# Two chained transformer blocks on one core: order of ScalarE's and VectorE's work in the second block's mixer

## What is computed

```python
h = _rmsnorm(x, norm_mix_g)
c_q, c_kv, k_r, x_m, z, i_pre, f_pre = _split_in(h @ w_in)
q  = (_rmsnorm(c_q, q_norm_g) @ w_uq)            # 8 heads, 64 + 32 rotated
kv = (_rmsnorm(c_kv, kv_norm_g) @ w_ukv)
attn_out = _mla_attention(q_nope, q_rope, k_nope, k_rope, v)
xc = silu(_causal_conv(x_m, conv_w, conv_b))
hm = _mlstm_chunkwise(xc @ w_mq, xc @ w_mk, x_m @ w_mv, ig, fg)   # 4 heads of 128
hm = (hm - mu) * rsqrt(var + EPS) * mh_norm_g
ml_out = (hm + ml_skip * xc) * silu(z)
x = x + concatenate([attn_out, ml_out]) @ w_o
x = x + _hier_moe(_rmsnorm(x, norm_ffn_g), ...)   # 32 experts, top 2
```

## Time and profile before

| | us |
|---|---|
| median of 3 runs | 1010.97 (1010.72 to 1012.38) |
| the profiled execution, own time | 1011.97 |
| its span, first to last instruction | 1010.4 |
| PE busy | 955.8 (95%) |
| DVE busy | 635.3 (63%) |
| ACT busy | 534.4 (53%) |
| mean granted PE clock | 0.991 |

### The profile page before, as it was taken

One profiled execution on the slowest core, in us unless ns is written; L12 is line 12 of the kernel. 1 busy time (PEld: TensorE's weight loads), 2 busy tenths in 40 slices (PEclk: granted clock), 3 DMA queues, 4 the chain that ended last, 5 costly groups with the idle time before them and its releaser, 6 DMA issues.

```text
span 1010.4 us, 14997 instructions
## 1 busy us (share of the span) xinstructions
PE 955.8 (95%) x5635; PEld 733.8 (73%) x5635; DVE 635.3 (63%) x1392; ACT 534.4 (53%) x973; POOL 84.1 (8%) x97
## 2 busy tenths in 40 slices
PE   6999899999999999999999999999899999987796
PEld 5777588888888877688888888867676665443355
DVE  4679768999945566768999945667876221110046
ACT  5757667676634565767666644765742211100054
POOL 0100001122100302001122101010000000000000
PEclk9999999999999999999999999999899999999998
DMA  8934246655565544246655664414577999999971
GB/s 272 384 131 126 91 125 200 202 177 180 200 204 173 203 146 146 84 138 197 204 171 188 199 184 142 149 48 167 209 305 306 396 419 420 421 420 421 421 280 44
DMA packets 99359, 224.58 MB, mean 222 GB/s; under 512 B 9535, under 2 KB 64210, under 8 KB 86994
## 3 DMA queue, kind: packets, MB, share of 16 engines
q1 hardware_dynamic: 99122, 223.04, 61.8%
q10 hardware_dynamic: 160, 0.53, 0.2%
HBM read 222.50 MB, written 1.05 MB: 221 GB/s over the span
## 4 chain that ended last, share of the span: by engine, by line
PE 76%; DMA 10%; DVE 8%; ACT 3%; SPq 2%; issue 1%; DVEq 0%; ACTq 0%
PE ps L559 72%; DMA ringx<-in_w_up_e_dram 6%; PE ps L563 3%; DMA ring<-in_w_up_e_dram 3%; DVE wl L1991 2%; DVE smb L2005 1%; DMA ring<-in_w_uv_dram 1%; SPq L2993 1%; SPq L2996 1%; DMA ring<-in_w_in_even_dram 1%; ACT L1443 1%; ACT wh L1446 0%; DVE pb L1996 0%; ACT hh L1443 0%; DVE x L1991 0%
## 5 line engine op out<-in xcount | busy, mean ns | idle before, releaser
L1991 DVE TENSOR_TENSOR wl<-ring,wh 128x1024 fp32r<-128x1024 f32 (+3 forms) x212 | 268.8, 1270 | 106.6 <-ACT wh L1446 105.3
L1446 ACT ACTIVATE wh<-ring 128x1024 fp32r<-128x1024 f32 (+3 forms) x212 | 222.2, 1051 | 105.6 <-PE ps L559 101.3
L559 PE MATMUL ps<-hx,wh 128*128 128x512 f32 (+1 forms) x720 | 245.0, 387 | 0.1
L559 PE MATMUL ps<-hx,wl 128*128 128x256 f32 x704 | 196.6, 280 | 0.0
L559 PEld LDWEIGHTS ps<-hx,wh 128*128 128x128 f32 x720 | 133.7, 187 | 28.8 <-issue 0.6
L559 PEld LDWEIGHTS ps<-hx,wl 128*128 128x128 f32 x704 | 133.1, 189 | 0.0
L559 PE MATMUL ps<-ring,xg 128*32 128x256 f32 (+1 forms) x592 | 79.4, 388 | 7.2 <-DMA ring<-in_w_gate_e_dram 4.2
L2938 POOL TENSOR_TENSOR fs<-fs,rt 128x256 f32<-128x256 f32 x44 | 52.4, 1213 | 357.1 <-ACT fs L1443 357.1
L559 PE MATMUL ps<-wh,hh 128*128 128x512 f32 (+3 forms) x192 | 79.7, 415 | 2.2 <-DVE wl L1991 2.1
L559 PE MATMUL ps<-wl,hh 128*128 128x512 f32 (+3 forms) x192 | 75.1, 391 | 0.0
L559 PE MATMUL ps<-wh,hl 128*128 128x512 f32 (+3 forms) x192 | 73.0, 388 | 0.0
(11 more groups left out here) (317 smaller groups left out, 1674.8 us busy)
## 6 DMA issues: line engine op xcount, KB each, us to landing
ring<-in_w_up_dram SPq DMA_DIRECT2D x88, 512.0 KB, 4.8
ring<-in_w_down_dram SPq DMA_DIRECT2D x22, 1024.0 KB, 5.0
ring<-in_w_up_e_dram SPq DMA_DIRECT2D x19, 1024.0 KB, 18.1
ring<-in_w_gate_e_dram SPq DMA_DIRECT2D x18, 1024.0 KB, 13.7
ring<-in_w_down_e_dram SPq DMA_DIRECT2D x15, 1024.0 KB, 26.0
ringx<-in_w_down_e_dram SPq DMA_DIRECT2D x14, 1024.0 KB, 21.0
ring<-in_w_in_odd_dram SPq DMA_DIRECT2D x12, 1024.0 KB, 5.2
ringx<-in_w_gate_e_dram SPq DMA_DIRECT2D x12, 1024.0 KB, 15.7
```

The lines of the kernel that those rows point to most:

```text
L559: return e.matmul(o, l, r, start=start, stop=stop)
L1446: return e.activation(o, i, ACT.Copy)
L1991: return e.tensor_tensor(o, a, b, op)
```

## The change

Four places of the mixer get another order; no instruction is added or taken away, and PE's own list stays as it is.

1. DVE: the split of X1 (`split_lo(c_in2[0] + 6)`) moves behind the first step of `side2`, the latent norm.
2. ACT: `swish(0)` moves behind the read-outs of `q2T`.
3. DVE, loop: the split of Z2 moves from step 0 to step 2. At step 11 the read-out of the mLSTM bank moves ahead of the split of O1. At step 13 `mix_lo` of the second latent output moves ahead of step 3 of the mLSTM norm.
4. ACT, loop: the silu of z moves from step 12 to step 11, the split of O2 from step 11 to 12 and that of O3 from step 13 to 14, `mix_hi` of the second latent output from behind the loop to step 13 ahead of the norm's root, and the scaling of the convolution by the skip gain from step 11 to 13 behind the root.

```diff
-            swish(0)
             for i in (1, 3):
                 evac(flat(qT3[0:96, 2 * i:2 * i + 2, :]), "q2T", i, rows=96)
+            swish(0)
...
                     copy(mix[:, 1, 512:1024], b[:, :]).then_inc(of(drained, "ml", 1), 1)
+                    for m in range(4):
+                        emptied(q, "z", m)
+                    act(szT[:, :, :], szT[:, :, :], ACT.Silu).then_inc(s_sz, 1)
+                if i == 12:
+                    next(outp)
+                if i == 13:
+                    warm()
+                    mix_hi("mla", 1, mla_hi[:, 1, :])
+                    q.wait_ge(s_var, RV["mln"])
+                    act(st[:, 16:24], st[:, 8:16], ACT.Sqrt).then_inc(s_std, 1)
                     q.wait_ge(s_xc, 2)
                     for h in range(4):
                         act(xcT[:, h, :], xcT[:, h, :], ACT.Copy, scale=gain("sk2", h))
-                if i == 12:
-                    for m in range(4):
-                        emptied(q, "z", m)
-                    act(szT[:, :, :], szT[:, :, :], ACT.Silu).then_inc(s_sz, 1)
-                    warm()
-                if i == 13:
-                    q.wait_ge(s_var, RV["mln"])
-                    act(st[:, 16:24], st[:, 8:16], ACT.Sqrt).then_inc(s_std, 1)
-                if i in out_at[2]:
-                    next(outp)
...
-            mix_hi("mla", 1, mla_hi[:, 1, :])
+                if i in (13, 14):
+                    next(outp)
+            next(outp)
...
             tok_evac("pj", pj[:, 0, :], "nm2", 424)
-            split_lo(c_in2[0] + 6, wh, wl)
...
             next(side)
+            split_lo(c_in2[0] + 6, wh, wl)
...
+                if i == 11:
+                    next(hms)
+                if i == 2:
+                    next(proj)
+                    next(proj)
                 if i and i - 1 in z_steps and i != 10:
                     next(proj)
                 if i == 11:
+                    next(proj)
+                if i == 12:
                     next(hms)
-                    next(proj)
-                if i in (12, 13):
+                if i == 13:
+                    mix_lo("mla", 1, mla_hi[:, 1, :], mla_lo[:, 1, :], 10)
                     next(hms)
-                if i == 14:
-                    mix_lo("mla", 1, mla_hi[:, 1, :], mla_lo[:, 1, :], 10)
                 if i == 0:
-                    next(proj)
-                    next(proj)
                     gate_rows(0)
```

## The result

| | before | after |
|---|---|---|
| median of 5 runs, us | 1011.13 (1010.72 to 1012.38) | 1015.82 (1012.52 to 1016.82) |
| ratio, 95% interval | | 1.0043 [1.0032, 1.0053] |
| the profiled execution, own time and span | 1011.97, 1010.4 | 1012.52, 1010.9 |

What follows compares the result with a forecast made beforehand. PE holds 76% of the chain of waits; from 766 us DMA is full. From 1011.97, 3.4 + 1.8 - 1.65 - 1.5 = plus 2.05 gave 1014.0; half of 1.00 off made 1013.5, range 1010.6 to 1016.4.

Steps and rivals of the forecast that it cites:

- X1, plus 3.4: At X1 behind the latent norm: PE waits 4.2 us for the later split, reaching the latents' transposes 3.4 us later.
- The rival in which PE finds X1 ready: At X1: the moved split isn't waited for, so the kernel gets faster, 1007.6 us; chance 0.03.
- The clock behind it, plus 1.8 between 0 and 3.05: Behind PE's wait at X1: the clock falls to half and costs 1.8 us, bounds 0 and 3.05.
- The rival in which the clock holds: At X1: no clock drop follows the wait, so the 1.8 us goes, 1011.7 us; chance 0.18.
- The swish, nothing: Silu behind the read-outs of q's transposes: no effect, as the silus run under PE's z product.
- Z2, minus 1.65: First loop steps: without DVE's 7.06 us stand, PE's second mLSTM score comes sooner, gaining 1.65 us, between 1.2 and 1.9.
- The half-limit: At the second mLSTM score: the moved Z2 split ends near 684.0, so the next maxima start about 0.25 us late.
- The loop's end, minus 1.5: Last value product to O4: PE's 2.89 us wait and its clock drop go, but the norm limits the gain to 1.5.
- The rival of a second drop: Ahead of O3 and O4: new waits of 1.3 and 1.9 us, clock drop adding 1.76 to 3.05, about 1015.9; chance 0.14.
- Paid in full: Loop's end: all 5.9 us kept instead of 1.5, DVE's O4 split near 721, 1009.1 or 1007.3 us; chance 0.08.
- The table loads: ACT's two switches: 1.28 us per load counted; the skill page's drains, 2.8 us more and near 1016, left out.
- One for one to the end: From 766 us the DMA engines are full, so every microsecond at PE's last mixer product reaches the end.

Runs made afterwards that it cites:

- only_x1_busy: Kernel before with only the split of X1 moved behind the latent norm, plus 32 extra products on PE ahead of X1; 1013.46 us, ratio 1.0030.
- only_x1: Kernel before with only the split of X1 moved behind the latent norm; 1017.26 us, ratio 1.0064.
- after_again: The whole change, unaltered, measured once more against the kernel before; 1014.20 us, ratio 1.0039.
- only_z2: Kernel before with only the split of Z2 moved from step 0 to step 2 of the loop; 1007.26 us, ratio 0.9972.
- only_swish: Kernel before with only `swish(0)` moved behind the read-outs of `q2T`; 1011.50 us, ratio 0.9998.
- only_end: Kernel before with only the reordering at the loop's end, on ACT and DVE; 1011.60 us, ratio 1.0008.
- undo_x1: The change with the split of X1 put back ahead of the latent norm, the other three edits kept; 1009.35 us, ratio 0.9985.
- after_busy: The whole change plus 32 extra products on PE ahead of X1; 1012.69 us, ratio 1.0013.
- only_end_keep: Kernel before with only the loop's end reordered, plus three more wide products on PE ahead of the router's; 1013.93 us, ratio 1.0031.

## Why the prediction was right, step by step

The forecast was slower, 1013.5 in a range of 1010.6 to 1016.4. The medians 1015.82 and 1014.20 lie in the range, 2.3 and 0.7 above the forecast. The direction is earned: X1 alone makes the kernel slower, and putting X1 back makes the change faster than before. That the sum comes so close is in part luck. By the medians of the kernels with one edit, X1 costs 6.44 (5.2 forecast with its clock), Z2 gains 3.56 (1.65), the loop's end costs 0.64 where it was to gain 1.5, the swish costs 0.54 (0); the last two are no change by their intervals. Two terms are off by about 2 us in opposite directions. The step that failed is the loop's end.

- *X1, plus 3.4*: right. only_x1_busy, with the clock kept up, has 3.36. The wait was 4.06 (4.2 forecast). The rival in which PE finds X1 ready falls.
- *The clock behind it, plus 1.8 between 0 and 3.05*: right in kind and near in size. It cost 2.33 in the first profile and in only_x1, and 4.86 - 3.36 = 1.5 in after_again, where the stretch was shorter. The rival in which the clock holds falls for these three executions. One reading behind this term was wrong: the trace of before does have a wait longer than 4.2 us before the experts, PE's first one, 6.26 us for a load at the start of the program. The products of 128x484 behind it take about 0.60 us each until 15 us and 0.38 from there on. The trace's record of the clock begins only at 15.15 us, so that wait could give the term no bound.
- *The swish, nothing*: right.
- *Z2, minus 1.65*: right. The first profile has 4.31 - 5.99 = -1.68 from z's first product, and only_z2 -1.74. The half-limit I worked out is there too: the second score at 688.33, the next maxima just behind the moved split.
- *The loop's end, minus 1.5*: the mechanism was wrong. The size was right up to 745 us, by luck (-1.62 in the first profile, -1.57 in after_again, from 712), and so was the order of the steps: against the shift of 3.84 that the stage started with, DVE took O4's split at 725.09 (725.08 before). ACT's four durations, added from 719.9, make 725.4 and not the 725.1 of the prediction; they overlap a little, and ACT was done at 728.89 - 3.84 = 725.05. But I put the gain down to the order, which brings 0.1 us. only_swish shows nearly all of the 1.6 without the new order, as the price of the drop at 719. And in only_end, undo_x1, after_busy and after_again the clock falls again at 745 to 752 and takes 1.7 back.
- *The rival of a second drop* was right about the new waits (1.3 and 1.9 us forecast, 1.05 and 1.61 measured), about the price (1.76 at its lower end, 1.7 measured) and the sequel, wrong in part about the place: behind O4's wait in undo_x1 alone, and in four kernels of the new order at the router, where PE waits just 0.4 us. I gave it 0.14, which was too little. With it and the measured clock, 3.36 + 2.33 - 1.68 - 1.6 + 1.7 = 4.1, against 4.7 and 3.4 measured.
- *Paid in full*: falls. It asked for DVE's O4 split near 721 us, and that split did not move.
- *The table loads*: the Trainium skill (ScalarE: Activation LUTs, section What ACT_TABLE_LOAD costs) adds a drain of about 1.38 us to a switch. The trace does not agree: after the loads at 715.52 and 719.59 the next instruction starts 1.29 and 1.30 us later, the load's own 1.28, and the copies ahead of the loads end at 715.50 and 719.58: no drain shows. That 1014 to 1016 came out is no evidence for it.
- *One for one to the end*: not borne out in single executions. From 766 to 990 us the shift changes by -1.4 us in the first profile, +0.4 in after_again and -2.6 in undo_x1, though the transfers fill that stretch. About 1.55 of it is the wait of 2.89 for one expert load that the profile of before has at 949.93, where most others have 1.3.

What stays open: where in a given execution the clock falls (before's own runs spread over 5 us, 1008.16 to 1013.22, in one set), and so the last 1 to 2 us of any sum here. The shift at 766 and the difference of the medians are up to 2.5 us apart (only_end_keep: +0.97 and +3.45), and the expert stage gives back 1 to 3 us in some profiles (only_z2: -3.01 at 766, -5.45 at 990) for reasons that no run here separates, but for the longer wait of before at 949.93.

## What to carry to other kernels

Before moving a piece of work behind something that gates one consumer, look at the order in which its own consumer stands in the waiting engine's list: here PE wanted X1 ahead of the latents, so 0.76 us gained for the latents cost 3.4 for X1. Price a TensorE wait of some us twice, once as the wait and once as the slow clock behind it, and tell the two apart by filling the wait with idle products. A gain that consists of a drop that goes away is kept only if the clock doesn't fall in a later stage instead; look for that stage in several executions, not in one.

## What was not expected of the hardware

Extra work made a kernel faster: 32 products in a wait, 4.08 us of PE's time, took 3.8 us off the median. The same wait of 2.89 us came with half clock for 6.8 us in before, for 3.4 in only_z2, only_x1 and only_x1_busy, and with none in only_swish. And the clock fell with PE busy almost throughout (11.60 of 12 us between 740 and 752 in only_end): what PE did ahead of that drop were 16 transposes and 32 products of 36 columns.
